# Attention in a two-layer trunk: softmax division on GpSimd, and a transposed-probability copy shared by ScalarE and VectorE

## What is computed

```python
def one_block(qi):                      # 128 queries at a time
    s = jnp.einsum('bqkgd,bskd->bkgqs', qi, kf) * scale
    p = jax.nn.softmax(s, axis=-1)
    return jnp.einsum('bkgqs,bskd->bqkgd', p, vf)
...
for i in range(DEPTH):                  # DEPTH = 2
    xp, k_i, v_i = trunk_layer(xp, cond_ctx, None, None, p)
    xs, _, _ = trunk_layer(xs, c, cache_k[:, i], cache_v[:, i], p)
```

## Time and profile before

| | |
|---|---|
| median of 3 runs | 1548.91 us (1543.1 to 1551.49) |
| profiled execution | 1550.63 us |
| span of that execution | 1548.7 us |
| TensorE busy | 1465.7 us, 95% |
| VectorE busy | 907.4 us, 59% |
| ScalarE busy | 519.4 us, 34% |
| GpSimd busy | 409.4 us, 26% |

### The profile page before, as it was taken

One profiled execution on the slowest core, in us unless ns is written; L12 is line 12 of the kernel. 1 busy time (PEld: TensorE's weight loads), 2 busy tenths in 40 slices (PEclk: granted clock), 3 DMA queues, 4 the chain that ended last, 5 costly groups with the idle time before them and its releaser, 6 DMA issues.

```text
span 1548.7 us, 25735 instructions
## 1 busy us (share of the span) xinstructions
PE 1465.7 (95%) x10321; PEld 1431.0 (92%) x10321; DVE 907.4 (59%) x1366; ACT 519.4 (34%) x744; POOL 409.4 (26%) x266
## 2 busy tenths in 40 slices
PE   6997789999999999999999978998999999999996
PEld 5997668989999999999999967898999999999996
DVE  0497895879683738695646577436944323444333
ACT  2424664252232113223223467425223211323221
POOL 1165100214342004243311530020433200333320
PEclk9999899999999999999999989998999999999998
DMA  8252021514343524343431200031422321222311
GB/s 318 86 164 85 29 68 38 170 50 155 122 132 120 152 72 146 109 151 111 138 94 49 72 28 2 15 97 47 157 68 81 94 70 56 81 68 81 94 57 69
DMA packets 191825, 147.02 MB, mean 95 GB/s; under 512 B 4337, under 2 KB 179065, under 8 KB 190713
## 3 DMA queue, kind: packets, MB, share of 16 engines
q1 hardware_dynamic: 191160, 145.51, 30.4%
q10 hardware_dynamic: 576, 0.26, 0.1%
HBM read 142.87 MB, written 2.88 MB: 94 GB/s over the span
## 4 chain that ended last, share of the span: by engine, by line
PE 87%; DVE 6%; ACT 2%; issue 2%; POOL 1%; DMA 1%; SPq 0%; DVEq 0%; ACTq 0%; POOLq 0%
PE pair L1076 69%; PE pair L1093 5%; PE pair L1341 3%; PE pair L1319 2%; PE pair L1159 2%; PE pair L1306 2%; PE pair L1192 2%; DVE mod_acc L805 1%; DVE small L969 1%; POOL tree L480 1%; DVE q_st L906 1%; ACT tree L692 1%; DVE w_lo L782 1%; PE pair L1146 1%; PE pair L1134 0%
## 5 line engine op out<-in xcount | busy, mean ns | idle before, releaser
L1076 PE MATMUL pair<-in_hi,w_hi 128*128 128x320 f32 x1792 | 411.7, 311 | 7.7 <-DVE w_lo L782 7.7
L1076 PE MATMUL pair<-in_hi,w_lo 128*128 128x320 f32 x1792 | 409.3, 310 | 0.0
L1076 PE MATMUL pair<-in_lo,w_hi 128*128 128x320 f32 x1792 | 408.8, 310 | 0.0
L1076 PEld LDWEIGHTS pair<-in_hi,w_hi 128*128 128x128 f32 x1792 | 300.2, 188 | 9.3 <-issue 6.3
L1024 DVE SCALAR_TENSOR_TENSOR conv<-pair,vec,conv 128x127 f32<-128x127 f32 x352 | 168.8, 541 | 236.3 <-ACT conv L720 236.1
L1076 PEld LDWEIGHTS pair<-in_lo,w_hi 128*128 128x128 f32 x1792 | 300.5, 188 | 0.0
L1076 PEld LDWEIGHTS pair<-in_hi,w_lo 128*128 128x128 f32 x1792 | 300.1, 188 | 0.0
L511 POOL TENSOR_TENSOR silu_a<-silu_a,conv 128x640 f32<-128x640 f32 x44 | 110.8, 2519 | 587.0 <-DVE conv L1024 587.0
L782 DVE TENSOR_TENSOR w_lo<-w_raw,w_hi 128x1024 fp32r<-128x1024 f32 (+1 forms) x152 | 203.8, 1342 | 82.9 <-ACT w_hi L532 82.7
L720 ACT ACTIVATE conv<-pair,vec 128x640 f32<-128x640 f32 x88 | 77.7, 885 | 438.1 <-PE pair L1076 427.4
L805 DVE SCALAR_TENSOR_TENSOR mod_acc<-mod_raw,cond,mod_acc 128x1024 f32<-128x1024 f32 x140 | 221.5, 1623 | 0.1
(11 more groups left out here) (146 smaller groups left out, 1600.9 us busy)
## 6 DMA issues: line engine op xcount, KB each, us to landing
w_raw<-in_w_up_dram SPq DMA_DIRECT2D x88, 512.0 KB, 3.9
mod_raw<-in_w_mod_dram SPq DMA_DIRECT2D x80, 512.0 KB, 4.1
w_raw<-in_w_down_dram SPq DMA_DIRECT2D x32, 704.0 KB, 4.7
w_raw<-in_w_in_dram SPq DMA_DIRECT2D x20, 512.0 KB, 4.2
w_first<-in_w_mod_dram SPq DMA_DIRECT2D x8, 1024.0 KB, 14.2
w_raw<-in_w_out_dram SPq DMA_DIRECT2D x16, 512.0 KB, 3.9
out_dram<-yout SPq DMA_DIRECT2D x5, 512.0 KB, 4.0
xin<-in_x_sample_dram SPq DMA_DIRECT2D x1, 2048.0 KB, 17.6
```

The costliest lines, as they stand in the source:

```text
L1076: ins = pe.matmul(dst[:, a:a + HALF_T], w[:, s, k, :], rhs[:, kk, a:a + HALF_T], start=first and r == 0, stop=last and r == 2)
```

## The change

1. VectorE no longer divides. GpSimd does, in both layers, for all 40 units, between the turning of the queries and the clearing of the sum. It waits for each reciprocal.
2. In layer 1, for units with 640 keys, ScalarE copies the first three key tiles of the transposed probabilities and VectorE the last two. VectorE's copy of unit i - 3 stands in step i, behind maximum and factor of unit i and ahead of the reciprocal of unit i - 1.
3. The transposes are written 128 columns further on in PSUM pair 2, so that three tiles lie in its first bank and two in its second.
4. TensorE's transposes and value products in layer 1 wait for a second semaphore as well, `s_pte_dve`.

```diff
+        PT0, PT_CUT = P, 3 * P
+        def vector_copies(L, i):
+            per_layer = NU - NH
+            if L == 0:
+                return 0
+            return (L - 1) * per_layer + (i if i <= NH else max(NH, i - NH))
+        def has_vector_copy(L, i):
+            return L > 0 and UNITS[i][0] != 0
...
@@ gpsimd, after the turning of the queries
+                for i in range(NU):
+                    nkeys = P if UNITS[i][0] == 0 else T
+                    pool.wait_ge(s_rec, L * NU + i + 1)
+                    pool.tensor_scalar(prob[i % 3][:, 0:nkeys], prob[i % 3][:, 0:nkeys], small[:, i % 3, 2:3], None,
+                                       ALU.mult).then_inc(s_prob, 1)
                 clear_sum(2 * L + 1)
...
@@ scalar
-                        act_e.activation(prob_place[j % 4][:, 0:nkeys], pair[2][:, 0:nkeys], ACT.Copy).then_inc(s_pte, 1)
+                        ncopy = PT_CUT if has_vector_copy(L, j) else nkeys
+                        act_e.activation(prob_place[j % 4][:, 0:ncopy], pair[2][:, PT0:PT0 + ncopy], ACT.Copy).then_inc(s_pte, 1)
...
@@ vector
-                for i in range(NU + 1):
+                for i in range(NU + 3):
...
-                    if i > 0:
+                    if i >= 3 and has_vector_copy(L, i - 3):
+                        un = L * NU + i - 3
+                        dve.wait_ge(s_pt, un + 1)
+                        if i >= 7:
+                            dve.wait_ge(s_o, un - 3)
+                        dve.tensor_copy(prob_place[(i - 3) % 4][:, PT_CUT:T],
+                                        pair[2][:, PT0 + PT_CUT:PT0 + T]).then_inc(s_pte_dve, 1)
+                    if 0 < i <= NU:
                         un, j = L * NU + i - 1, (i - 1) % 3
-                        nkeys = P if UNITS[i - 1][0] == 0 else T
                         dve.wait_ge(s_exp, un + 1)
                         dve.reciprocal(small[:, j, 2:3], small[:, j, 1:2]).then_inc(s_rec, 1)
-                        dve.wait_ge(s_rec, un + 1)
-                        dve.tensor_scalar(prob[j][:, 0:nkeys], prob[j][:, 0:nkeys],
-                                          small[:, j, 2:3], None, ALU.mult).then_inc(s_prob, 1)
...
@@ tensor
                     if i > 0:
                         pe.wait_ge(s_pte, un)
+                        if L > 0:
+                            pe.wait_ge(s_pte_dve, vector_copies(L, i))
...
-                        ins = pe.transpose(pair[2][:, kt * P:(kt + 1) * P], prob[i % 3][:, kt * P:(kt + 1) * P], ident)
+                        ins = pe.transpose(pair[2][:, PT0 + kt * P:PT0 + (kt + 1) * P],
+                                           prob[i % 3][:, kt * P:(kt + 1) * P], ident)
...
                     pe.wait_ge(s_pte, un + 2)
+                    if L > 0:
+                        pe.wait_ge(s_pte_dve, vector_copies(L, i + 2))
```

## The result

The changed kernel takes 1553.01 us (median of 20 runs, 1550.02 to 1554.36), the kernel before 1548.99 us in 20 runs beside it (1543.1 to 1553.3). The ratio is 1.0029 with a 95% interval of [1.0018, 1.0041]: a small loss, 4.5 us by this ratio and 4.0 by the medians, where 4 us of gain were forecast. It lies within the 0.5% and the range that the prediction named, but on the other side of no change.

A forecast was written before the change was run, and what follows sets the result against it. It took layer 0's attention as bound by VectorE's queue, layer 1's mostly by TensorE waiting for ScalarE's copy. Layer 0 -6.1 and layer 1 +1.9 gave -4.2 from 1548.9, so 1545 us, range 1540 to 1563.

The forecast's parts named there:

- M: Price of one division of 640 columns on GpSimd: taken as 0.9 us, with 0.72 and 1.56 as the ends.
- L975 held until GpSimd's instruction is over: VectorE's product of maximum and factor, 0.16 us, was expected to stop until GpSimd's running instruction ends.
- 1.7 + 2M: VectorE's loop for a pair with modulation in layer 0: 3.5 us at M = 0.9, against 4.37 now.
- Units 24 to 39 of layer 0, -1.4: Eight pairs in layer 0 were to come down by 0.17 us each, to TensorE's limit of 4.20.
- Units 16 to 24 of layer 0, -3.3: Four pairs in layer 0 were to take 0.82 us less each.
- The rest of layer 0, -1.4: The other 2.9 us by which layer 0's stage exceeds layer 1's; half was counted as gain.
- Layer 1, the copy behind the maximum: VectorE's half of the copy queues behind the maximum: +0.11 us a pair, +1.3 over twelve pairs.
- X: Distance from a pair's first transposes to its second in layer 1: 1.59 us before, 1.70 forecast.
- Layer 1, units 16 to 24, +1.0: VectorE-bound units in layer 1 were to cost M + 0.84 = 1.74 us each, against 1.60.
- The end of layer 1, -0.4: Last three units, where TensorE waits for copies alone, were to gain 0.21 us each less one.
- rival (b): Layer 0 doesn't gain, as modulation and divisions take turns; layer 1 pays its 1.9: 1550 to 1551 us, chance 0.16.
- Rival (a): Slower, L975 blocked by a long division in both layers' pair loops: +17.5, 1566 us at M = 1.56, chance 0.22.

The follow-up runs named there:

- e4: The changed kernel with GpSimd copying the 640 columns in place instead of dividing them: 1548.67 us, ratio 0.9988.
- e12: The changed kernel with GpSimd multiplying the probabilities by a constant tensor (two tensor inputs) instead of dividing: 1557.93 us, ratio 1.006.
- e7: The changed kernel, but in layer 0 GpSimd divides even units and VectorE odd ones; layer 1 as before, copy not split: 1553.58 us, ratio 1.002.
- e14: The changed kernel with GpSimd copying only 8 columns instead of dividing: 1550.88 us, ratio 0.9995.
- e6: The kernel before, with the modulation steps inside layer 0's attention cut to 32 of 1024 columns: 1545.19 us, ratio 0.9963.
- e5: The changed kernel, with the modulation steps inside layer 0's attention cut to 32 of 1024 columns: 1546.68 us, ratio 0.9987.
- e2: The changed kernel without the split copy; GpSimd divides in both layers, ScalarE copies all tiles: 1551.49 us, ratio 1.0014.
- e3: The changed kernel with the division back on VectorE in both layers, the copy in layer 1 still split: 1552.54 us, ratio 1.0015.

## Why the prediction was wrong, point by point

- **M = 0.9, ends 0.72 and 1.56: wrong, and the step that failed.** Measured 1.88, outside both ends. The nearest rows were a cast with no arithmetic and a subtraction with no per-partition operand; the upper end was taken as a bound because a second tensor seemed the dearest thing an instruction could have. The prediction named "over 1.4 us" as what would prove it wrong, and it did. It isn't the whole miss. With 0.72 us in its place (e4) the two stages take 169.61 us, 2.7 less than after (172.28) but only 0.85 less than before, where 4.2 were forecast; what is missing then is in the sum for layer 0 (third to fifth point).
- **L975 held until GpSimd's instruction is over: wrong for this instruction.** It is held for the first 0.8 us only (172.45 to 173.25, 918.70 to 919.50), and is rarely caught at all (8 times in 80). The two errors work against each other. The loop "1.7 + 2M" would give 5.46 us a pair at M = 1.88 and a loss of some 7.5 us in units 24 to 38; measured were 31.27 / 7 = 4.47. GpSimd works beside VectorE, not in series with it. In the earlier trace rows GpSimd's instruction was a product of two tensors, which in e12 does hold to its end, and the one stopped was a TENSOR_SCALAR like VectorE's division in e7. The row's times were read rightly and carried over to instructions of another kind.
- **Units 24 to 39 of layer 0, -1.4: lost.** 24 to 38 are 0.47 longer, not 1.2 shorter. With a cheap instruction (e4, e14) they are 0.67 shorter, so the gain forecast was about half there and the division's length turned it around.
- **Units 16 to 24 of layer 0, -3.3: over-sized and lost.** +0.23 measured, at a lower clock (0.82 against 0.95), -1.57 with GpSimd nearly free. The 0.82 for a pair isn't worked out in the prediction (its own 4.37 - 3.5 is 0.87), and it had taken the whole difference to a loop without gaps. The modulation step stays ahead of every second maximum and keeps part of it (e14). Without the modulation the old kernel itself takes 14.59 (e6).
- **The rest of layer 0, -1.4:** 1.3 less was measured in units 0 to 16, but 1.0 of it is the clock, as unchanged code shows, so little of it can be the change.
- **Layer 1, the copy behind the maximum: right.** X was forecast as 1.70 and measured as 1.71, the pair +0.11 and +0.11. Units 24 to 38: 7 x 0.11 = 0.77 forecast, 30.19 - 29.40 = 0.79 measured, and the same with GpSimd's step at 0.72 or 0.19 us (30.19, 30.20). Units 0 to 16 can't be read for it (28.37 in after, 29.93 in e5 with the same code).
- **Layer 1, units 16 to 24, +1.0: +0.89, and +0.73 at full clock (e5).** The number came out by luck: with M at 1.88 the formula M + 0.84 would have given 2.72 us a unit and +9. e2 and e3 show that either part alone brings most of it (+0.63, +0.86).
- **The end of layer 1, -0.4: +0.2.** The copy's part was right, -0.33 in e3 and with a cheap GpSimd (9.34, 9.33). In the kernel after TensorE waits for the division there: in e2, where the copy isn't split, the end is longer by 0.1.
- **The outcome** is nearest to rival (b), chance 0.16, though 1553 is above its 1550 to 1551: layer 0 hardly gains and layer 1 pays its 1.9 (2.3 measured). Its reason, that modulation and divisions take turns, is half of it; the other half is the division's own length, which (b) didn't have. Rival (a) had a long division, though not long enough, and wrongly multiplied it: 1566 was forecast for M = 1.56. That 1553 lies inside the range of 1540 to 1563 is luck: two errors worked against each other.

## What to carry to other kernels

Moving work off a full engine is worth what the new place leaves over: here 0.47 us of VectorE's queue became 1.88 on GpSimd, two of which with a wait behind the modulation (4.72 us in the worst pairs, 29.09 of 31.27 us over seven) leave no room in the 4.40 that a pair took. Before sizing such a move from nearby rows, measure that very instruction on that engine once, with its kind of scalar. When a copy is split between two engines, look at what stands ahead of each half in its queue: the half that comes last sets the time, and 0.21 us of gain on one became 0.11 of loss through a maximum on the other. And compare stages part by part, with the clock of each part: unchanged code differed by 1.7 us over a stage (88.09 to 89.79), and by 0.02 in the part where the clock was steady.

## What the runs showed of the hardware that was not expected

- On GpSimd a product of 128x640 with a per-partition scalar takes 1.88 us; with a whole tensor 1.55; a copy 0.72; and a copy of 8 columns 0.19. It reads half of what the product of two tensors reads, and is slower. The Trainium skill (GPSIMD Engine Reference, Engine selection) calls one-input work roughly line-rate against VectorE; the 0.72 us of the copy are not far from the 0.55 that VectorE takes for the division, the 1.88 us of GpSimd's division are 3.4 times that.
- A VectorE instruction with two SBUF inputs is held by this division for its first 0.80 us alone (ends at 173.25, 919.50), by a two-input product of 1.55 us to its end (208.19 to 209.08).
- It goes the other way as well: behind a VectorE instruction of 1.28 us with two SBUF inputs, GpSimd's copy of 8 columns takes 1.17 instead of 0.19, and its division 2.84 instead of 1.88. VectorE's division, 1.07 us into GpSimd's, makes that 2.19 long and isn't held itself; 1.27 to 1.39 us into it, it is the one that waits (e7).
- The span of one and the same kernel moves by 9 us with its mean granted clock (1549.7 at 0.976, 1540.8 at 0.984), which is as much as the largest difference measured here (e12).
